# Kernel study: an attention stage's modulation chunks summed side by side in one PSUM bank, and at the head TensorE spreads the modulation rows over the partitions

## The reference

```
mod_l = split(silu(c)     @ ada_w[layer] + ada_b[layer], 6)
mod_c = split(silu(c_ctx) @ ada_w[layer] + ada_b[layer], 6)
p     = (rmsnorm(x, norm_mix_g) * (1 + mod[1]) + mod[0]) @ w_in      # both streams
y     = concat(mla(p), windowed(p), neighbourhood(p), retention(p)) * mix_beta
x     = x + mod[2] * (y @ w_out)
h     = rmsnorm(x, norm_ffn_g) * (1 + mod[4]) + mod[3]
x     = x + mod[5] * peer_ffn(h)                                    # 128 experts a token, gathered
```

## Time and profile before

| what | value |
|---|---|
| median of 3 runs | 4947.29 us (4945.28 to 4955.01) |
| profiled execution, its own time | 4945.98 us |
| its span | 4944.2 us |
| mean granted clock of TensorE | 0.811 |
| PE, DVE, ACT, POOL busy | 3247.7, 3128.9, 913.5, 1495.9 us |
| DMA | 1496.72 MB, 303 GB/s on average |

### The profile page before, as it was taken

The page is one execution under the profiler, slowest core; times in us unless marked ns, Lnnn a source line. Parts: engine busy times, 40 slices in busy tenths (PEclk is TensorE's granted clock), DMA queues, the critical chain, the costliest instruction groups (busy, mean ns, idle before and its releaser), DMA issues.

```text
span 4944.2 us, 48806 instructions
## 1 busy us (share of the span) xinstructions
PE 3247.7 (66%) x16212; PEld 1259.8 (25%) x16212; DVE 3128.9 (63%) x8329; ACT 913.5 (18%) x2479; POOL 1495.9 (30%) x1376
## 2 busy tenths in 40 slices
PE   5888899665787555455545558898887545555545
PEld 2345445331232111111111114655332111111111
DVE  1242323687877878778777861523378787877876
ACT  1242311111111111111111121421111111111211
POOL 0000000334343443444444430000034444444443
PEclk7889998787897777877787778898888787777777
DMA  4132321799999999999999971011299999999998
GB/s 150 62 120 86 124 69 64 306 414 410 408 418 415 403 416 405 418 417 404 418 415 404 412 299 45 1 34 39 87 416 390 416 411 414 404 418 414 401 420 342
DMA packets 290749, 1496.72 MB, mean 303 GB/s; under 512 B 25432, under 2 KB 83928, under 8 KB 126656
## 3 DMA queue, kind: packets, MB, share of 16 engines
q0 software_dynamic: 185888, 1347.13, 66.3%
q1 hardware_dynamic: 73680, 114.85, 6.9%
q10 hardware_dynamic: 30928, 31.61, 1.9%
HBM read 1482.91 MB, written 10.58 MB: 302 GB/s over the span
## 4 chain that ended last, share of the span: by engine, by line
DVE 39%; PE 30%; DMA 19%; issue 7%; ACT 4%; POOL 1%; DVEq 0%; ACTq 0%; POOLq 0%; SPq 0%
DMA X<-in_uv_dram,X 18%; DVE X L1599 16%; PE ps L458 9%; PE ps L852 5%; DVE X L1610 2%; PE ps L627 2%; PE ps L819 2%; PE ps L668 2%; ACT X L1217 2%; DVE X L1516 1%; DVE X L1518 1%; DVE X L1519 1%; DVE X L1606 1%; PE ps L639 1%; PE ps L706 1%
## 5 line engine op out<-in xcount | busy, mean ns | idle before, releaser
L852 PE MATMUL ps<-X 64*64 64x512 f32 x2560 | 1640.1, 774 | 1408.9 <-DVE X L1610 1404.7
L1720 POOL DMA_INDIRECT X<-in_uv_dram,X x1280 | 1420.5, 1110 | 2167.9 <-PE ps L855 1629.3
L1599 DVE CUSTOM_DVE_ANT_0 X<-yT,X 128x1024 f32<-128x1024 f32 x1280 | 1532.9, 1223 | 340.2 <-DMA X<-in_uv_dram,X 306.8
L853 PE MATMUL ps<-X 64*64 64x512 f32 x2560 | 1640.2, 774 | 0.0
L855 PE MATMUL ps<-X 64*64 64x512 f32 x2560 | 1640.2, 774 | 0.0
L854 PE MATMUL ps<-X 64*64 64x512 f32 x2560 | 1640.2, 774 | 0.0
L852 PEld LDWEIGHTS ps<-X 64*64 64x64 f32 x2560 | 360.1, 163 | 2621.2 <-DVE X L1610 1972.8
L1217 ACT ACTIVATE X<-X 128x1 f32<-128x1 f32 x1280 | 258.6, 203 | 2338.4 <-DVE X L1599 2315.7
L855 PEld LDWEIGHTS ps<-X 64*64 64x64 f32 x2560 | 360.4, 163 | 0.0
L854 PEld LDWEIGHTS ps<-X 64*64 64x64 f32 x2560 | 360.3, 163 | 0.0
L853 PEld LDWEIGHTS ps<-X 64*64 64x64 f32 x2560 | 360.2, 163 | 0.0
(11 more groups left out here) (245 smaller groups left out, 3438.4 us busy)
## 6 DMA issues: line engine op xcount, KB each, us to landing
wring<-in_ada_w_dram SPq DMA_DIRECT2D x48, 1024.0 KB, 5.4
wring<-in_w_in_dram SPq DMA_DIRECT2D x24, 1024.0 KB, 5.5
wring<-in_peer_wq_dram SPq DMA_DIRECT2D x24, 1024.0 KB, 25.6
X<-in_uv_dram,X POOLq DMA_INDIRECT x1280
wring<-in_w_out_dram SPq DMA_DIRECT2D x8, 1024.0 KB, 5.1
X<-scores ACTq DMA_DIRECT2D x64, 128.0 KB
X<-mods ACTq DMA_DIRECT2D x15, 512.0 KB, 8.6
yT<-mods ACTq DMA_DIRECT2D x8, 512.0 KB, 9.1
```

The costliest lines, as they stand in the source:

```text
L852: pe.matmul(ps[0:HD, h, :], dg(slice(0, HD), s), v0[0:HD], **ends)
L853: pe.matmul(ps[HD:P, 2 + h, :], dg(slice(HD, P), s), v0[HD:P], **ends)
L1599: v.tensor_tensor_reduce(uvr[:, slot, 0:D], h2[:, t, :], uvr[:, slot, 0:D], 1.0, 0.0, ALU.mult, ALU.add, adot[:, s_:s_ + 1]).then_inc(S("d ...
L1720: g.indirect_dma_start(uvr[:, slot, :], None, a["uv"], bass.IndirectOffsetOnAxis(ap=istages[i % 2][:, s:s + 1], axis=0)).then_inc(S(f"uv{s ...
```

## The change

**Late chunks.** `cT` gets 14 zero columns ahead of the two that hold values. Chunk i of an attention stage takes the 32 columns that begin at 14 - 2i, so its two rows fall on partitions 2i and 2i + 1 of each quarter, and all chunks of a stage are accumulated into one bank: eight chunks in `mla` (pairs 0, 1, 3, 4, 6, 7, 9, 10), six each in `swa` and `na` (even pairs), none in retention. Once a stage, after pair 10, ScalarE copies the bank, one `late_sum` adds the quarters of up to 16 rows (`picks`) and the biases (a small matrix `bias_to`), and `late_out` copies and stores them with two transfers. The order of the weights follows.

**Head.** For each chunk TensorE multiplies the copied bank with `pick_wide`, which repeats a row's picking column 128 times, and adds the bias by a row of 128 ones: the result is the row repeated over the partitions, for each of the two streams, in banks 0 to 3. ScalarE copies the shift rows into the tables (`head_shift`), VectorE makes the scale tables out of PSUM. The gain is loaded at the beginning. Chunks 0 to 3 are not stored in DRAM and not loaded back. The wait for `picked` moves from before the first product to the first spread.

The core of the diff:

```diff
-MOD_PAIRS = (0, 2, 4, 6, 8, 10)
-MOD_KINDS = {"mla": MOD_LATE[0:6], "swa": MOD_LATE[6:12], "na": MOD_LATE[12:18]}
-MOD_LAST = MOD_LATE[18:]
+MOD_ORDER = ("mla", "swa", "na")
+MOD_PAIRS = {"mla": (0, 1, 3, 4, 6, 7, 9, 10), "swa": (0, 2, 4, 6, 8, 10), "na": (0, 2, 4, 6, 8, 10)}
+MOD_KINDS = {"mla": (0, MOD_FIRST, 8), "swa": (1, 0, 6), "na": (1, 6, 6)}
+MOD_MOST = 8
+MOD_WIDE = 2 * (MOD_MOST - 1)
...
-                    after = {1: mod[0:12], 3: mod[12:18], 5: mod[18:]}
+                    after = {1: mod[0:14], 3: mod[14:20]}
...
+                def head_modulation():
+                    def spread(c):
+                        pe.wait_ge(S("mpc"), c + 1)
+                        if c == 2:
+                            pe.wait_ge(S("mtab"), 1)
+                        if c == 3:
+                            pe.wait_ge(S("mtab"), 2)
+                        pe.wait_ge(S("picked"), 1)
+                        for s in range(2):
+                            pe.matmul(ps[:, 2 * (c % 2) + s, :], pick_wide[:, s, :], mrow[:, c % 2, :], start=True, stop=False)
+                        pe.wait_ge(S(f"ab{c % 2}"), 16 * (c // 2 + 1))
+                        for s in range(2):
+                            m = pe.matmul(ps[:, 2 * (c % 2) + s, :], ones_wide[0:1, :], adab[0:1, c % 2, :], start=False, stop=True)
+                        m.then_inc(S("mps"), 1)
+                    for c in range(MOD_FIRST):
                         if c >= 2:
-                            pe.wait_ge(S("mrow"), B("mrow", M) + c - 1)
+                            pe.wait_ge(S("mpc"), c - 1)
...
+                        if c:
+                            spread(c - 1)
+                    spread(MOD_FIRST - 1)
-                def late_parts(M, c):
-                    pe.wait_ge(S("mrow"), B("mrow", M) + c)
+                def late_parts(kind, i):
+                    b = MOD_ORDER.index(kind)
+                    if i == 0 and b:
+                        pe.wait_ge(S("brow"), b)
+                    at = MOD_WIDE - 2 * i
                     for half in range(2):
                         g = take(1)
                         for j in range(GROUP_K):
-                            m = pe.matmul(ps[32 * j:32 * j + 32, 6, :], cT[:, half * GROUP_K + j, :], wring[:, g % WRING, j, :],
-                                          start=(half == 0), stop=(half == 1))
+                            m = pe.matmul(ps[32 * j:32 * j + 32, 6, :], cT[:, half * GROUP_K + j, at:at + 32], wring[:, g % WRING, j, :],
+                                          start=(i == 0 and half == 0), stop=(i == len(MOD_PAIRS[kind]) - 1 and half == 1))
...
+                def late_sum(kind):
+                    b, n_ = MOD_ORDER.index(kind), len(MOD_PAIRS[kind])
+                    pe.wait_ge(S("bpc"), b + 1)
+                    pe.matmul(ps[0:2 * MOD_MOST, 6, :], picks, mod_late[0], start=True, stop=False)
+                    pe.wait_ge(S("bb"), 16 * (b + 1))
+                    pe.matmul(ps[0:2 * MOD_MOST, 6, :], bias_to[0:n_, :], mod_late[1][0:n_, :], start=False, stop=True).then_inc(S("bps"), 1)
...
-                            if L < LAST and p in MOD_PAIRS:
-                                late_parts(*MOD_KINDS[kind][MOD_PAIRS.index(p)])
-                            if L < LAST and p - 1 in MOD_PAIRS:
-                                late_sum(*MOD_KINDS[kind][MOD_PAIRS.index(p - 1)])
+                            if L < LAST and p in MOD_PAIRS[kind]:
+                                late_parts(kind, MOD_PAIRS[kind].index(p))
+                            if L < LAST and p - 1 == MOD_PAIRS[kind][-1]:
+                                late_sum(kind)
...
-                if L < LAST:
-                    late_parts(*MOD_LAST[0])
                 for t in range(TILES):
-                    if L < LAST and t == CT:
-                        late_sum(*MOD_LAST[0])
...
-                if L < LAST:
-                    late_parts(*MOD_LAST[1])
-                    late_sum(*MOD_LAST[1])
-                    pe.wait_ge(S("mrow"), B("mrow", L + 1) + ADA_CHUNKS)
...
+                def head_rows(c):
+                    act.wait_ge(S("mpp"), c + 1)
+                    if c >= 2:
+                        act.wait_ge(S("mps"), c - 1)
+                        load_bias(c)
+                    nc.scalar.activation(mrow[:, c % 2, :], ps[:, 6 + c % 2, :], ACT.Copy).then_inc(S("mpc"), 1)
+                def head_shift(c):
+                    act.wait_ge(S("mps"), c + 1)
+                    for s in range(2):
+                        m = nc.scalar.activation(norm_tables[0][0][:, 2 * s + 1, c * CH:(c + 1) * CH], ps[:, 2 * (c % 2) + s, :], ACT.Copy)
+                    m.then_inc(S("mtab"), 1)
...
                 if L == 0:
-                    load_bias(0, 0)
-                    load_bias(0, 1)
-                    modulation(0, range(2), MOD_FIRST)
+                    load_bias(0)
+                    load_bias(1)
+                    act.dma_start(norm_tables[0][1], a["norm_mix_g"][0:1, :].partition_broadcast(P).rearrange("a b c -> a (b c)")).then_inc(S("gain"), 16)
+                    head_rows(0)
+                    head_rows(1)
+                    head_shift(0)
                     act.wait_ge(S("in"), 16 * 7)
                     squares(0, range(TILES))
-                    modulation(0, range(2, MOD_FIRST), MOD_FIRST)
+                    head_rows(2)
+                    head_shift(1)
+                    head_rows(3)
...
-                    load_tables(0, 0, MOD_FIRST)
                     norm(0, range(TILES))
...
+            v.wait_ge(S("gain"), 16)
+            for c in (2, 3):
+                v.wait_ge(S("mps"), c + 1)
+                for s in range(2):
+                    at = slice((c - 2) * CH, (c - 1) * CH)
+                    m = v.scalar_tensor_tensor(norm_tables[0][0][:, 2 * s, at], ps[:, 2 * (c % 2) + s, :], 1.0, norm_tables[0][1][:, at], ALU.add, ALU.mult)
+            v.wait_ge(S("mtab"), 2)
+            m.then_inc(S("n_scale"), 1)
```

More of the change, by code:

```diff
@@ L284, in build @@
         cE = view(100 * K + 32, [KD, 2])
-        pick = ones[:, 2:4]
+        cT = view(96 * K, [KD, MOD_WIDE + 32])
+        picks = view(98 * K, [2 * MOD_MOST]); bias_to = view(98 * K + 2 * MOD_MOST, [2 * MOD_MOST])
         qm = view(0, [HEADS, TOK]); km = view(12 * K, [HEADS, TOK]); vm = view(24 * K, [TILES, GW])
@@ L308, in build @@
         ptab = sb("ptab", [P, 2 * P + 8])
+        pick_wide = view(84 * K, [2, P]); ones_wide = view(85 * K, [P])
         krrow = view(69 * K, [TILES, MLA_QK])
@@ L318, in build @@
         pabf = view(86 * K + 144, [2, TOPK]); sel = view(86 * K + 176, [2, TOPK]); gs = view(86 * K + 208, [2, PH])
[L320 to L327, removed]
+        mod_late = (yT[:, 6, 0:CH], yT[:, 7, 0:CH])
         h2 = yT[:, :, :].rearrange("p a b -> p (a b)").rearrange("p (t d) -> p t d", d=D)
@@ L487, in modulation @@
                             for j in range(GROUP_K):
-                                m = pe.matmul(ps[32 * j:32 * j + 32, 6 + c % 2, :], cT[:, half * GROUP_K + j, :], wring[:, g % WRING, j, :],
+                                m = pe.matmul(ps[32 * j:32 * j + 32, 6 + c % 2, :], cT[:, half * GROUP_K + j, MOD_WIDE:MOD_WIDE + 32], wring[:, g % WRING, j, :],
                                               start=(half == 0), stop=(half == 1))
                             m.then_inc(S("mpp" if half else "w_half"), 1)
[L491 to L494, removed]
-                def late_parts(M, c):
-                    pe.wait_ge(S("mrow"), B("mrow", M) + c)
+                        if c:
[6 more added lines that the diff above has]
+                    at = MOD_WIDE - 2 * i
                     for half in range(2):
@@ L514, in _ @@
                     pe.wait_ge(S("silu"), 1)
-                    pe.wait_ge(S("picked"), 1)
-                    modulation(0, range(MOD_FIRST))
+                    head_modulation()
                     pe.wait_ge(S("in"), 16 * 7)
@@ L943, in squares, with load_tables @@
                         nc.scalar.activation(stat[:, 1, t:t + 1], stat[:, 0, t:t + 1], ACT.Sqrt, scale=1.0 / D, bias=eps[:, 0:1]).then_inc(S("n_rt"), 1)
-                def load_tables(M, tag, chunks):
-                    for q in range(2):
-                        act.wait_ge(S(f"ms{q}"), B(f"ms{q}", M) + 16 * (chunks // 2))
+                def load_tables(M, tag):
+                    act.wait_ge(S("bst"), 32 * (3 if M else 1))
                     tabs, gain = norm_tables[tag]
@@ L974, in _ @@
                 else:
-                    load_tables(0, 0, MOD_FIRST)
                     norm(0, range(TILES))
-                for q in range(2):
-                    act.wait_ge(S(f"ms{q}"), B(f"ms{q}", L) + 16 * ((ADA_CHUNKS if L else MOD_FIRST) // 2))
-                if L < LAST:
-                    load_bias(*MOD_LATE[0])
+                    act.wait_ge(S("mps"), MOD_FIRST)
+                    load_late_bias(MOD_ORDER[0])
                 act.wait_ge(S("kr"), B("kr", L) + 1)
```

(15 more changed lines are left out.)

98 lines of the change are left out of this document (37 added, 61 removed).

## The result

The changed kernel takes 4908.4 us in the median of 4 runs (4896.4 to 4909.9) against 4947.6. The ratio is 0.9914, 95% interval 0.9901 to 0.9926: 39 us less, within the forecast range and 9 short of the forecast. A second job ran the same file four times more: 4893.0 to 4911.5, median of all eight 4907.8. The profiled execution took 4909.85 (span 4908.0), so the span is 36.2 us shorter, where 47.5 were forecast.

What follows compares the result with a forecast made beforehand. No engine alone was taken as the bound: the chain is split between VectorE, TensorE and DMA. Savings of 12.1 + 5.8 + 14.4 + 9.5 + 2 + 3.75 = 47.5 us gave 4899.8 us, range 4889 to 4911 (69%).

Steps and rivals of the forecast that it cites:

- Head: 12.1 forecast: Head: scaled tables done at 59.0 instead of 71.1, a gain of 12.1 us, bounds 6.5 and 15.
- The gain load: Head: a 0.52 MB load moved to the front, counted as a cost of 1.0 us, bounds 0 and 1.4.
- the eight matmuls: Head, spreads of the last two chunks: 4.3 us at half clock, then 5.6 at full; all at half 14.4.
- First stage: 5.8 forecast: First attention stage: five sums go (9.5 us), two products come (3.7), net 5.8 us gained.
- third: 9.5: Third attention stage: five sums leave the chain, 13.2% of 72 us, a gain of 9.5 us.
- other work at half clock: Attention stages: matmuls around the removed sums speed up if sums hold the clock down; 2 us, bounds -6 and +10.
- Second stage: 14.4 forecast: Second attention stage: five sums go, 2.9 us each, mostly at half clock, 14.4 us; lower bound 9.5 at full clock.
- Retention: 3.75 forecast: Retention: one product step and one sum ahead of the state updates go, 1.85 + 1.9 = 3.75 us.
- (a): Rival, three attention stages: most half-clock stretches vanish, some 12 us more; 4888 or less, down to 4875; 12%.
- (b): Rival: head matmuls all at half clock, late weights, second-stage sums worth only 9.5; 4911 to 4918; 10%.
- (c): Rival, attention stages: ScalarE's wait takes the sums' place, only head and retention gain, 16 us; 4932; 4%.
- (d): Rival, first attention stage: thinner TensorE work falls to half clock, a loss of 60 us; 4960; 2%.

Runs made afterwards that it cites:

- Squares last: Changed kernel with ScalarE's six squares after the four row copies of the head instead of between them; 4896.0 us.
- head filler: Changed kernel with 8 more unread 256-column matmuls in the head, between chunk 3's products and the wait for ScalarE; 4907.6 us.
- head only: Kernel before with only the head of the change, its 20 sums kept; 4935.9 us.
- filler: One unread 256-column matmul per layer 0 attention item, in TensorE's wait for ScalarE's rows; 4884.2 us on the changed kernel, 4925.0 on the kernel before.
- late only: Changed kernel with the head of before, so only the late chunks are changed; 4917.7 us.
- narrow weights: Changed kernel with an unread 256-column matmul per layer 0 attention item, through weights 2 columns wide; 4889.1 us.
- filler of 2 columns: Changed kernel with an unread matmul of 2 columns instead of 256 per layer 0 attention item; 4911.2 us.
- filler in stages 1 and 3: Changed kernel with the unread 256-column matmul per item only in layer 0's first and third attention stages; 4900.0 us.

## Why the prediction held, and what it missed

The mechanism was right: the table loads leave the head, the sums leave the chain, and what stood behind them moves forward. The sizes were less good than the total. The profiled execution gave 36.2 us of the 47.5 forecast, and 3.2 of the 36.2 came from the part where nothing changed. That the median lies within the range owes something to such luck.

*Head: 12.1 forecast, 7.9 measured at the scaled tables.* Each step was near: chunk 1 done at 31.1 (31.8), its spread at 35.7 (36.5), the third spread started at 46.97 (48.1). The gain load moved chunk 1's last weights by 0.3 us in this pair of profiles, where 1.0 was counted. Over all profiles they came at 28.5 to 28.9 with the head of before and at 29.1 to 30.1 with the new one, 0.7 later by the medians. By the Trainium skill's rule of shared DMA engines (Trainium Kernel Development and Optimization, Key Constraints) it should have cost up to 1.4; the traces lie between nothing and that. The mis-sized term is the eight matmuls: 9.6 forecast with 4.3 us at half clock, 14.9 measured, all at half clock, where the forecast's own bound had 14.4. Squares last and head filler show the same matmuls at 1.98 us for two instead of 3.78 once TensorE doesn't idle before them.

*First stage: 5.8 forecast, 2.7 measured; third: 9.5 and 6.3.* The chain was read rightly: a pair without late work is 1.9 us shorter, and no wait took the sum's place (TensorE's wait for ScalarE's rows is 34.6 us over 28 waits, before 37.1 over 31). What failed is the term "other work at half clock", for which I counted a gain of 2 us, on the idea that narrow sums hold the clock down. The clock fell instead. In the third stage it did so with either head: 0.90 (before) and 0.87 (head only) with the sums, 0.83 in all five profiles without the sums and without filler in the stage. In the first it depends on the head: 0.94 to 0.90 from head only to the changed kernel, but 0.94 to 0.93 from before to late only, and there the stage gave 5.6 us, nearly the 5.8 forecast. So the missing 3 us of the first stage are lost to the clock, but that the removal alone lowered it is not shown; something else sets it too. With the filler in both kernels, so with the clock held, the change is worth 95.3 - 89.9 = 5.4 and 85.5 - 76.1 = 9.4, near the forecast terms. The other fillers have 89.1 to 91.1 and 77.6 to 78.8 for these stages, so 9.4 is the upper end of 6.7 to 9.4.

*Second stage: 14.4 forecast, 12.2 measured.* With the clock held it is 96.0 - 87.8 = 8.2, where the bound at full clock had been 9.5. The 14.4 took each sum at the half clock at which it ran. In the changed kernel the clock is as low as before (0.74), and most of that comes back, not all. Head only has the sums of before and took 107.8, from which the changed kernel is only 8.4 away: part of the 12.2 is not the change's doing.

The three stages gave 21.1 where the sum with its clock term said 31.7, and 23.0 with the clock held. So in this pair of profiles the clock cost the change only some 2 us net, less than the 7.4 by which one late code varies. The forecast's excess was in counting both the slow sums and a gain in clock.

*Retention: 3.75 forecast, 5.9 measured.* 1.8 of the excess is TensorE's clock at the start of the projections (0.98 before, 1.00 after). The projections after the second stage lost the same 1.8 (1.00 to 0.98). Neither was forecast; together they are nothing.

*Rivals.* (a), the clock lifts: fell, and its reason was turned round. (b) named three losses: the head at half clock, which came true (5.3 us in the matmuls, 4.2 in the end), five sums of the second stage worth only 9.5, which the pair with the clock held bears out (8.2), and late weights, of which the chain shows none. The total, 4908.4, lies between the forecast and its 4911 to 4918. (c) fell with the 6.9 us pairs. (d) named a mechanism that did appear, thinner work lets the clock fall, and was right in sign but not in size: up to 0.04 and 0.07 of clock and not 0.35. Its price was off as well, for 84.57 to 160 us is a loss of 75 and not 60. The rule beside it, that gaps make bursts start at half rate (the Trainium skill, TensorE: Matmul & The Clock Gate, HAM oscillation), the trace bears out in part: with work in the gaps the clock rose and three stages took 19.6 us less, but without it the first stage still had 0.90, so not every burst started slow.

*The range.* The prediction says that the bounds of its terms give 4885 to 4914. Added up, all at the worst or all at the best, they give 4920 and 4889.

Open: what decides when the clock comes back in the head. Seven profiles have the unaltered new head, and all idle for 3.8 us before the spreads. In three (filler, filler of 2 columns, filler in stages 1 and 3; first norm 58.8 to 59.6) two matmuls ran slow and the other six at full clock. In two (head only, narrow weights; 63.1 and 63.3) six ran mostly slow and the last two at full clock. In both of the changed kernel (63.6 and 63.4) all eight were slow. In the attention stages, too, it isn't known what decides: the head filler's kernel begins them 4 us earlier than the changed one and has each within 0.1 us of it. Open too is how much of the 18 us between executions of one program comes from such cases. The weights' timing in adjacent pairs was not tried by itself.

## What to carry to other kernels

Work taken off the critical chain comes back by its place in the chain, but count it at full clock (23.0 us here against 31.7) and ask what it did for the clock: in these runs even a useless matmul through narrow weights raised it. Where TensorE waits a microsecond or so again and again in short items, a matmul that nobody reads, placed in the wait and shorter than it, can be worth about as much as the work that was optimised away (here 19.6 us against 21.1 in the three stages). One profile a kernel is not enough to judge such a stage: the same late code differed by 7.4 us from one profile to another. At the head of a kernel, order the engine that feeds TensorE so that its short copies come ahead of long work that is needed later.

## What the runs showed of the hardware that I had not expected

A matmul of 256 columns through weights 2 columns wide held the clock as well as one through 128: 0.95, 0.94, 0.93 against 0.95, 0.92, 0.96; one of 2 columns did nothing (0.92, 0.75, 0.82). After a fall, unbroken work brought the clock back within 3.9 us in three heads, some 10 us after the fall in two (with a gap of 0.3 us in the work) and not within 14.9 us in two, with the same instructions. The same program varied by 18 us, 0.4%, from execution to execution; the filler kernel by 9.
